# Moving one weight tile by 192 bytes in a two-block transformer kernel on one Trainium2 core

## What is computed

```python
# first block
x = x + 0.5 * swiglu(rms_norm(x), w_gate, w_up, w_down)      # 1024 -> 2816 -> 1024
proj = rms_norm(x) @ w_in                                     # q, k, v, index heads, pool input
x = x + concat(sparse_attention(...), pooled(...)) @ w_out
x = x + 0.5 * swiglu(rms_norm(x), ...)
# second block
x = x + 0.5 * swiglu(rms_norm(x), ...)
z = rms_norm(x) @ w_in_2                                      # 1024 -> 7168
x = x + (sigmoid(g_a) * y_a + sigmoid(g_b) * y_b) @ w_out_2
x = x + 0.5 * swiglu(rms_norm(x), ...)
out = rms_norm(x)
```

## Time and profile before

| | |
|---|---|
| median of 3 runs | 1077.28 us |
| profiled execution, its own time | 1077.27 us |
| its span, first to last instruction | 1075.4 us |
| granted TensorE clock | 0.999 of full speed |
| PE busy | 1064.2 us (99%) |
| DVE busy | 773.2 us (72%) |
| ACT busy | 615.9 us (57%) |
| POOL busy | 180.4 us (17%) |
| DMA | 200.53 MB, mean 186 GB/s |

### The profile page before, as it was taken

How to read it: one execution, slowest core, us unless ns; L and a number is a source line. 1 busy time by engine, 2 the same in 40 slices (tenths; PEclk the granted TensorE clock), 3 DMA queues, 4 the chain that set the end, 5 groups by cost and what they waited for, 6 DMA issues and landing times.

```text
span 1075.4 us, 17556 instructions
## 1 busy us (share of the span) xinstructions
PE 1064.2 (99%) x6120; PEld 931.6 (87%) x6120; DVE 773.2 (72%) x1111; ACT 615.9 (57%) x940; POOL 180.4 (17%) x196
## 2 busy tenths in 40 slices
PE   8999999999999999999999999999999999999997
PEld 6888888888888888888888888889988888888885
DVE  6866666799787666668666666787777778676553
ACT  6755544466765554447555545755655556555642
POOL 3411100120211111001111101133201021111100
PEclk9999999999999999999999999999999999999999
DMA  8755555554366555555555554656555556655552
GB/s 293 266 186 194 188 186 178 172 181 163 96 210 197 188 184 184 187 191 194 186 191 195 177 194 158 216 179 196 165 193 182 188 182 201 199 192 193 169 187 77
DMA packets 55714, 200.53 MB, mean 186 GB/s; under 512 B 6320, under 2 KB 6320, under 8 KB 55536
## 3 DMA queue, kind: packets, MB, share of 16 engines
q1 hardware_dynamic: 54288, 195.58, 55.1%
q0 software_dynamic: 656, 3.18, 0.8%
q10 hardware_dynamic: 720, 1.09, 0.3%
HBM read 198.78 MB, written 1.05 MB: 186 GB/s over the span
## 4 chain that ended last, share of the span: by engine, by line
PE 97%; ACT 1%; DVE 1%; DMA 1%; issue 0%; ACTq 0%; DVEq 0%
PE pair L1380 42%; PE pair L1381 22%; PE pair L1402 10%; PE pair L1374 5%; PE pair L1375 5%; PE pair L1376 5%; PE pair L1404 5%; DMA x<-x_in 1%; PE pair L1763 0%; PE pair L1468 0%; PE pair L1696 0%; PE pair L1683 0%; PE pair L1627 0%; PE pair L1674 0%; ACT qk_a L670 0%; ACT x_hl L460 0%
## 5 line engine op out<-in xcount | busy, mean ns | idle before, releaser
L838 DVE TENSOR_TENSOR w_lo<-w_raw,w_hi 128x1024 fp32r<-128x1024 f32 x369 | 460.1, 1251 | 228.3 <-ACT w_hi L453 227.4
L453 ACT ACTIVATE w_hi<-w_raw 128x1024 fp32r<-128x1024 f32 x369 | 386.4, 1057 | 252.5 <-PE pair L1381 199.5
L1380 PE MATMUL pair<-x_hl,w_hi 128*128 128x512 f32 x1408 | 491.0, 394 | 2.6 <-DVE x_hl L844 2.5
L1381 PE MATMUL pair<-x_hl,w_lo 128*128 128x256 f32 x1408 | 394.2, 280 | 0.0
L1380 PEld LDWEIGHTS pair<-x_hl,w_hi 128*128 128x128 f32 x1408 | 263.8, 187 | 62.0 <-issue 3.2
L1381 PEld LDWEIGHTS pair<-x_hl,w_lo 128*128 128x128 f32 x1408 | 266.5, 189 | 0.2
L1380 PE MATMUL pair<-wide,w_hi 128*128 128x512 f32 x592 | 205.8, 392 | 0.0
L1381 PE MATMUL pair<-wide,w_lo 128*128 128x256 f32 x592 | 166.2, 281 | 0.0
L368 POOL TENSOR_TENSOR wide<-side,wide 128x256 fp32r<-128x256 f32 x88 | 86.6, 984 | 384.1 <-ACT wide L511 384.1
L1380 PEld LDWEIGHTS pair<-wide,w_hi 128*128 128x128 f32 x592 | 110.9, 187 | 24.4
L1381 PEld LDWEIGHTS pair<-wide,w_lo 128*128 128x128 f32 x592 | 112.3, 190 | 0.0
(11 more groups left out here) (209 smaller groups left out, 1110.5 us busy)
## 6 DMA issues: line engine op xcount, KB each, us to landing
w_raw<-stream SPq DMA_DIRECT2D x369, 512.0 KB, 3.3
const<-const_in POOLq DMA_DIRECT2D x1, 1248.0 KB, 7.5
w_raw<-stream SPq DMA_DIRECT2D x4, 256.0 KB, 5.6
rows<-rows_in POOLq DMA_DIRECT2D x1, 576.0 KB, 9.5
x<-x_in ACTq DMA_DIRECT2D x2, 256.0 KB, 5.6
x<-x_in SPq DMA_DIRECT2D x2, 256.0 KB, 6.4
sgu_w<-sgu_w_in POOLq DMA_DIRECT2D x1, 512.0 KB, 12.6
qk_a<-gain_in POOLq DMA_DIRECT2D x1, 512.0 KB, 3.8
```

Of the source, the lines that this page charges most:

```text
L453: nc.scalar.activation(w_hi[:, slot, :], w_raw[:, slot, :], ACT.Copy).then_inc(w_hi_done, 1)
L838: nc.vector.tensor_tensor(w_lo[:, slot, :], w_raw[:, slot, :], w_hi[:, slot, :].bitcast(F32), ALU.subtract).then_inc(w_split, 1)
L1380: nc.tensor.matmul(dst, a_hi, b_hl.rearrange("p a s -> p (a s)"), start=first, stop=False, skip_group_check=True)
L1381: return nc.tensor.matmul(dst[:, 0:S], a_lo, b_hl[:, 0, :], start=False, stop=last, skip_group_check=True)
```

## The change

Two unused tiles are declared, one ahead of `w_hi` of 48 floats (192 bytes) and one ahead of `w_lo` of 16 floats (64 bytes).

```diff
 LEAD_ROOM = 96
+HIGH_ROOM = 48
+LOW_ROOM = 16
 CONST_ROOM = 2560
...
         w_raw = sb("w_raw", [P, RING, BW])
+        sb("high_room", [P, HIGH_ROOM])
         w_hi = sb("w_hi", [P, RING, BW], F32R)
+        sb("low_room", [P, LOW_ROOM])
         w_lo = sb("w_lo", [P, RING, BW], F32R)
```

## The result

The changed kernel takes 1069.95 us, the median of six runs from 1066.90 to 1073.23, beside 1077.29 us before (the median of six executions); the ratio is 0.993 with a 95% interval of 0.9916 to 0.9943. Three of the six lie at 1066.9 to 1068.3 and three at 1071.6 to 1073.2. The profile was taken of one at 1073.23 us (span 1071.4).

The account below looks back on a forecast made before the run. PE was taken to bound the kernel, by matmul count times spacing; 0 (DMA) + 0 (splits) + 0 (matmuls) against the profiled 1077.27 us gave a forecast of 1077.3 us, range 1055 to 1091.

Parts of the forecast that it names:

- The bound: Whole kernel: PE busy 1064.2 of 1075.4 us, so the time is the count of matmuls times their spacing.
- the rows on `conv_in`: Operations reading 0, 4 or 8 bytes off, used for the splits: at most 1% slower, 12 ns a split, hidden; cost zero.
- the price of an offset in the matmuls: Matmuls reading `w_hi` beside a read of another tile: a different start place costs zero, within 1 ns a matmul.
- the sum: DMA, splits and matmuls, each put at 0, against the profiled execution's 1077.27 us.
- the index stage: Six matmuls per chunk, moving row 0, 16 and 32 bytes off: 147, 148 and 147 ns each, so offset costs nothing.
- The faster rival: Matmuls reading `w_hi`: load and stream collide, 64 bytes apart removes it; 18.5 us less, 1059 us; chance 0.31.
- The slower rival: Pairs outside the slow windows: the slow cadence spreads, 346.5 to 353.6 ns, 13 us more, 1090 us; chance 0.23.
- My two slow windows: Pairs at 287.8 to 297.7 and 861.9 to 881.7 us: 353.6 ns, 7 ns a pair more, without a wait.

Follow-up runs that it names:

- e3_by_128: Kernel before the change with only the high-weight tile `w_hi` moved, 128 bytes off modulo 256 from the activations: 1089.03 us, ratio 1.0108.
- e8_back_32: Kernel before the change with only the high-weight tile `w_hi` moved, 32 bytes back modulo 256 from the activations: 1083.83 us, ratio 1.0059.
- e5_both_back: Kernel before the change with both weight tiles, high and low, 64 bytes back modulo 256 from the activations: 1087.28 us, ratio 1.0081.
- e4_low_back: Kernel before the change with only the low weight tile `w_lo` 64 bytes back modulo 256 from the activations: 1084.30 us, ratio 1.0060.

## Why the prediction was wrong

**The bound** was read right. PE's spacing sets the time, and no DMA or split took its place: PE's waits stayed near 3 us, and the splits within 2 ns, as the rows on `conv_in` had it.

**The step that failed** is the price of an offset in the matmuls, "From this row the price of an offset is zero, within 1 ns a matmul". It stands as 0 in the sum; by it the profiled executions moved by -4.0 and -10.0 us. I took the index stage for all forms, because there the moving rows lie 0, 16 and 32 bytes off. After the change, pairs measured -6.5 ns in one cadence and +3.7 in the other, the token form with 512 weights +7.4 a matmul, and runs 0. The index stage itself hardly answers to any placement: from start to start its matmuls take 147.4 ns before, 148.8 after the change, and 149.3 at the most (`e3_by_128`). Other forms do, at 32 bytes already: in `e8_back_32` the high matmuls of runs take 5 ns more and the token form 6.6. So the row could speak neither for other forms nor for 64 bytes, and the prediction knew of the second. The token loss, 3.7 us, had no place in my sum or in any rival.

**The faster rival** had the sign and, for the low matmul of a pair, the place: in the window from 310 us that one went from 117 to 113 ns. Its mechanism fell: it put 5.5 us on the runs, which didn't move (228.8 ns beside 228), and 5 us of gain on moving weights, which lost; it left the high matmul of a pair alone, which gained 3 ns (230 to 227); and `e5_both_back`, where all loads differ from their streams, should have been its best case and is 0.8% slower than before.

The Trainium skill, TensorE: Matmul & The Clock Gate, section Step-by-step: what each phase is for, says that loading the next tile doesn't steal read bandwidth from the running matmul. `e5_both_back` does not speak against it, as a plain collision of the two reads does not account for its 353.3 ns a pair. But the same instructions take 340 to 353 ns a pair, depending on where the tiles lie, and no run here shows which reads make the difference.

**The slower rival** described something real. Pairs do have a second, slower cadence, and all five other placements that moved a weight tile against the activations by less than 256 bytes were slower than before, by 0.6 to 1.1%. Its argument against itself, that the cadence does not depend on place because the same tiles run at both, was half right: one place does run at two cadences, but the place sets which ones. My two slow windows were the sign of it, and I used them as a bound only. They are parts of two whole stretches at 353.4 ns, 287 to 298 and 860 to 894 us, with 126 pairs in place of the 86 that I counted, and behind the plain fp32 matmuls of line 1468 at the end of each the pairs run at 346.5: what precedes a stream was to be seen before the change.

**Open.** What in the reads of loads and streams makes these sets, and why 64 back mostly enters the faster cadence and 64 forward mostly the slower one, is not settled. Neither "load against stream" nor "load against load" survives `e4_low_back` and `e5_both_back`. What costs the token form its time is open too, and so is the period. Reads and writes of the splits beside TensorE are an unlikely cause: in the window from 310 us every pair of the changed kernel takes 340 ns, though VectorE is busy for only 66.8 of its 90 us.

## What to carry to other kernels

Where TensorE bounds and its waits are near zero, read the start-to-start spacing of each form of stream, window by window, and compare it within one kernel: a stream of equal work at two spacings means that there is time to be had without changing any work. The place of the operands' tiles against each other, by 32 or 64 bytes, is then worth a scan, by measurement and form by form, since the same move can help pairs and hurt moving weights; the order of the products can take part of that loss back. Profile such a kernel more than once, because what precedes a stream, or a wait inside it, can choose its spacing.

## What the runs showed of the hardware

- With equal instructions, clock and waits, fp32r pairs of 512 and 256 columns ran at 340 to 353 ns, by the place of three tiles against each other and by how the stream began. In the steady windows all intervals of one stream keep one pattern, over hundreds of matmuls: all 265 intervals in the window from 310 us of the changed kernel are 340 ns.
- The cadence changed inside a stream at a wait of PE of 0.56 us (340 to 350 ns). And one plain fp32 matmul ahead of a stream changed it against the kernel without it (353 to 347, 350 to 340, and 340 to 350).
- A move of all operands of TensorE together, by 256 or by 192 bytes, changed nothing: 1077.27 us twice.
- Plain fp32 matmuls were not put to the test: the operands of line 1763 moved together. 32 of them took 3.5 us from first to last start before and after the change.
